# Modulation of both layers in the first phase of a two-layer diffusion trunk

## The reference

```python
def _adaln(cond, ada_w, ada_b):
    m = jax.nn.silu(cond) @ ada_w + ada_b          # (1024,) @ (1024, 6144)
    return jnp.split(m[:, None, :], 6, axis=-1)
...
for i in range(DEPTH):                              # DEPTH = 2
    sh1p, sc1p, g1p, sh2p, sc2p, g2p = _adaln(c_ctx[None, :], ada_w[i], ada_b[i])
    sh1s, sc1s, g1s, sh2s, sc2s, g2s = _adaln(c, ada_w[i], ada_b[i])
```

## Time and profile before

| | |
|---|---|
| median of three runs | 4691.73 us (4690.29 to 4693.51) |
| profiled execution, span | 4690.2 us |
| the profiled execution's own time beside its span | not given apart; the three runs are 0.1 to 3.3 us above the span |
| TensorE busy | 4009.3 us (85%) |
| VectorE busy | 1621.5 us (35%) |
| first phase, up to the first load of norm 0 | 125.2 us |
| route of layer 0, first load to first expert matmul | 1105.64 to 1287.24 us |
| route of layer 1, first load to first expert matmul | 3678.74 to 3825.10 us |

### The profile page before, as it was taken

The page is one execution under the profiler, slowest core; times in us unless marked ns, Lnnn a source line. Parts: engine busy times, 40 slices in busy tenths (PEclk is TensorE's granted clock), DMA queues, the critical chain, the costliest instruction groups (busy, mean ns, idle before and its releaser), DMA issues. The chain is left out here.

```text
span 4690.2 us, 56580 instructions
## 1 busy us (share of the span) xinstructions
PE 4009.3 (85%) x22791; PEld 3241.3 (69%) x22791; DVE 1621.5 (35%) x2557; ACT 926.8 (20%) x1606; POOL 582.8 (12%) x446
## 2 busy tenths in 40 slices
PE   8599798977799999995999956877888649999996
PEld 1599543454299999995999943444444549999995
DVE  3432355443600010014125546566666351000101
ACT  0423202013111111114123322111111301111112
POOL 0000000000200010000001103343344001000100
PEclk9699797987899999997999977888888669999998
DMA  6422201046667787753222255111110538778774
GB/s 222 158 66 62 105 11 50 15 160 250 224 235 271 274 274 260 269 180 112 85 73 84 65 180 202 45 45 49 63 50 27 192 105 278 256 268 282 259 271 172
DMA packets 342007, 732.47 MB, mean 156 GB/s; under 512 B 17220, under 2 KB 59708, under 8 KB 335986
## 3 DMA queue, kind: packets, MB, share of 16 engines
q1 hardware_dynamic: 306028, 625.59, 37.5%
q0 software_dynamic: 27168, 99.25, 7.6%
q10 hardware_dynamic: 8719, 6.51, 0.5%
HBM read 635.71 MB, written 95.59 MB: 156 GB/s over the span
## 5 line engine op out<-in xcount | busy, mean ns | idle before, releaser
L1608 PE MATMUL moe_banks<-moe_xt,mix_ring 128*128 128x144 f32 x8192 | 1012.7, 287 | 3.3 <-ACT moe_xt L1646 3.3
L1608 PEld LDWEIGHTS moe_banks<-moe_xt,mix_ring 128*128 128x128 f32 x8192 | 1009.0, 191 | 4.0 <-issue 3.5
L1623 PE MATMUL moe_banks<-moe_hid,mix_ring 128*128 128x144 f32 x4096 | 510.3, 287 | 0.0
L1623 PEld LDWEIGHTS moe_banks<-moe_hid,mix_ring 128*128 128x128 f32 x4096 | 503.5, 191 | 0.9
L1671 DVE TENSOR_TENSOR moe_hid<-moe_banks,moe_sg 128x144 f32<-128x144 f32 x256 | 78.8, 308 | 921.9 <-ACT moe_sg L1657 921.9
L62 PE MATMUL ssdin_banks<-h_leading,ssdin_w_split 128*128 128x384 f32 x1920 | 385.8, 335 | 5.8 <-ACT ssdin_pad L1867 2.9
L62 PEld LDWEIGHTS ssdin_banks<-h_leading,ssdin_w_split 128*128 128x128 f32 x1920 | 337.4, 188 | 7.2 <-issue 7.0
L1657 ACT ACTIVATE moe_sg<-moe_banks 128x144 f32<-128x144 f32 x256 | 74.3, 290 | 964.0 <-PE moe_banks L1608 964.0
L2553 DVE SCALAR_TENSOR_TENSOR scan_exp<-scan_exp,scan_rates,scan_cb 128x128 f32<-128x128 f32 x576 | 240.4, 490 | 56.4 <-ACT scan_exp L2444 55.9
L2346 PE MATMUL scan_banks<-scan_w,scan_yc 128*128 128x512 f32 x576 | 251.9, 599 | 4.4 <-DVE scan_yc L2596 4.4
L62 PE MATMUL hyin_banks<-h_leading,hyin_w_split 128*128 128x384 f32 x1152 | 235.5, 339 | 19.2 <-DVE hyin_w_split L575 18.9
(11 more groups left out here) (335 smaller groups left out, 4602.3 us busy)
## 6 DMA issues: line engine op xcount, KB each, us to landing
mix_ring<-in_moe_w_gate SPq DMA_DIRECT2D x64, 2048.0 KB, 7.8
mix_ring<-in_moe_w_up SPq DMA_DIRECT2D x64, 2048.0 KB, 12.9
mix_ring<-in_moe_w_down SPq DMA_DIRECT2D x64, 2048.0 KB, 9.3
mod_w<-in_ada_w SPq DMA_DIRECT2D x12, 2048.0 KB, 7.9
mix_ring<-in_ada_w SPq DMA_DIRECT2D x12, 2048.0 KB, 15.9
ssdin_w<-in_ssd_in_w SPq DMA_DIRECT2D x10, 2048.0 KB, 9.9
scan_xbc<-xbc_dram SPq DMA_DIRECT2D x9, 1536.0 KB, 7.0
st_xb<-xbc_dram SPq DMA_DIRECT2D x10, 1280.0 KB, 7.1
```

What stands on the lines that cost most here:

```text
L1608: ins = pe.matmul(pb[:, 2 * (f % 2) + j, 0:SLOTS], ring[:, 2 * half + j, k, col:col + P], xt[:, k, :], start=(k == 0), stop=(k == KD - 1))
L1623: ins = pe.matmul(pb[:, d % 4, 0:SLOTS], ring[:, 4 + half, k, col:col + P], hid[:, k, :], start=(k == 0), stop=(k == KD - 1))
```

## The change

Both layers' modulation is computed in the first phase. Its ring has six buffers instead of three. The 24 products are written out one after another in three banks, always in partitions 0 and 1; a product waits for the bank that the product three before it used, and filter layer 1 runs behind product 8. The rows of layer 0 are in partitions 0 and 1 and those of layer 1 in partitions 32 and 33 of the same tile, into which the bias is loaded first. Layer 0's rows are stored when all pieces have been issued, layer 1's behind its last piece; four read-backs follow, with four transposes and four column copies. `NextModulation` is gone and the route of layer 0 is the code of the route of layer 1.

```diff
--- before.py
+++ after.py
@@ -117,18 +117,20 @@
 def phase_modulation(nc, io, keep):
     ada = io["ada_w"].rearrange("l (k p) n -> p l k n", p=P)
-    RING = 3
+    RING = 6
     COLUMNS = 6 * D // HALF
+    ALL = 2 * COLUMNS
+    BANKS = (1, 2, 3)
+    FIRST = 9
     with ExitStack() as ctx:
         m = Mem(nc, ctx, "mod_")
         cond_rows = m.sb("cond_rows", [16, P])
         cond_t = keep["cond_t"]
         w = m.sb("w", [P, RING, KD, HALF])
-        bias = m.sb("bias", [2, 6 * D])
-        rows = m.sb("rows", [2, 6 * D])
-        a_row = m.sb("a_row", [2, D])
-        gain = m.sb("gain", [2, D])
-        mrows = m.sb("mrows", [48, 2, P])
+        rows = m.sb("rows", [34, 6 * D])
+        a_row = m.sb("a_row", [34, D])
+        gain = m.sb("gain", [34, D])
+        mrows = m.sb("mrows", [48, 4, P])
         stage = m.sb("stage", [P, 4, P])
         filt = Filter(m, io, keep["filt"])
         pb = m.psum()
@@ -147,28 +149,38 @@
         s_tr = m.sem("param_transposed")
         s_done = m.sem("params_kept")
+        def of_layer(tile, layer):
+            return tile[32 * layer:32 * layer + 2, :]
+
         with nc.Block() as block:
             @block.sync
             def _(sp):
+                def piece(n):
+                    layer, col = n // COLUMNS, n % COLUMNS
+                    sp.dma_start(w[:, n % RING, :, :], ada[:, layer, :, col * HALF:(col + 1) * HALF]).then_inc(s_w[n % RING], 16)
                 sp.dma_start(cond_rows[0:8, :], io["c_ctx"].rearrange("(k p) -> k p", p=P)).then_inc(s_c, 16)
                 sp.dma_start(cond_rows[8:16, :], io["c"][0].rearrange("(k p) -> k p", p=P)).then_inc(s_c, 16)
                 filt.load(sp)
-                for r in range(RING):
-                    sp.dma_start(w[:, r, :, :], ada[:, 0, :, r * HALF:(r + 1) * HALF]).then_inc(s_w[r], 16)
-                with sp.Fori(1, COLUMNS // RING) as i:
-                    for r in range(RING):
-
-                        sp.wait_ge(s_acc, i * RING + (r - RING + 1))
-                        sp.dma_start(w[:, r, :, :], ada[:, 0, :, bass.ds((i * RING + r) * HALF, HALF)]).then_inc(s_w[r], 16)
-                sp.wait_ge(s_row, COLUMNS)
-                sp.wait_ge(s_arow, 1)
-                modulation_out(sp, io, 0, rows, a_row, mrows, s_out, s_back)
+                for n in range(ALL):
+                    if n >= RING:
+                        sp.wait_ge(s_acc, n - RING + 1)
+                    piece(n)
+                for layer in range(2):
+                    sp.wait_ge(s_row, COLUMNS * (layer + 1))
+                    sp.wait_ge(s_arow, layer + 1)
+                    modulation_out(sp, io, layer, of_layer(rows, layer), of_layer(a_row, layer), s_out)
+                for layer in range(2):
+                    sp.wait_ge(s_out, 2 * 5 * 16)
+                    for c in range(2):
+                        sp.dma_start(mrows[:, 2 * layer + c, :], io["mod_dram"][layer, c].rearrange("(r p) -> r p", p=P)
+                                     ).then_inc(s_back, 16)
             @block.scalar
             def _(act):
-                modulation_in(act, io, 0, bias, gain, s_bias)
+                for layer in range(2):
+                    modulation_in(act, io, layer, of_layer(rows, layer), of_layer(gain, layer), s_bias)
                 for n, (src, at, cnt) in enumerate(keep["param_rows"]):
                     act.dma_start(stage[at[1]:at[1] + cnt, at[0], :], src).then_inc(s_stage, 16)
                 for h in range(2):
@@ -184,53 +196,68 @@
             @block.tensor
             def _(pe):
+                def product(n):
+                    pe.wait_ge(s_w[n % RING], 16 * (n // RING + 1))
+                    if n >= len(BANKS):
+                        pe.wait_ge(s_row, n - len(BANKS) + 1)
+                    for k in range(KD):
+                        ins = pe.matmul(pb[0:2, BANKS[n % len(BANKS)], :], cond_t[:, k, :], w[:, n % RING, k, :],
+                                        start=(k == 0), stop=(k == KD - 1))
+                    ins.then_inc(s_acc, 1)
+
                 pe.wait_ge(keep["s_const"], 16)
                 pe.wait_ge(s_c, 32)
                 pe.transpose(pb[:, 0, 0:16], cond_rows[:, :], keep["ident"][0:16, 0:16]).then_inc(s_ct, 1)
                 pe.wait_ge(s_silu, 2)
-                for layer in range(2):
-
-                    filt.products(pe, pb, layer)
-                    with pe.Fori(layer * COLUMNS // RING // 2, (layer + 1) * COLUMNS // RING // 2) as i:
-                        for r in range(RING):
-
-                            pe.wait_ge(s_w[r], i * 16 + 16)
-
-                            pe.wait_ge(s_row, i * RING + (r - RING + 1 if layer else 0))
-                            for k in range(KD):
-                                ins = pe.matmul(pb[0:2, 1 + r, :], cond_t[:, k, :], w[:, r, k, :],
-                                                start=(k == 0), stop=(k == KD - 1))
-                            ins.then_inc(s_acc, 1)
+                filt.products(pe, pb, 0)
+                for n in range(FIRST):
+                    product(n)
+                filt.products(pe, pb, 1)
+                for n in range(FIRST, ALL):
+                    product(n)
                 pe.wait_ge(filt.s_arg, 2)
                 pe.wait_ge(s_stage, 16 * (len(keep["param_rows"]) + 2))
                 for n, cnt in enumerate(keep["param_counts"]):
                     pe.transpose(pb[:, 4 + n // 4, (n % 4) * P:(n % 4) * P + cnt], stage[0:cnt, n, :],
                                  keep["ident"][0:cnt, 0:cnt]).then_inc(s_tr, 1)
-                pe.wait_ge(s_back, 32)
-                for c in range(2):
+                pe.wait_ge(s_back, 64)
+                for c in range(4):
                     pe.transpose(pb[:, 6, c * P:c * P + 48], mrows[:, c, :], keep["ident"][0:48, 0:48]).then_inc(s_tr, 1)
             @block.vector
             def _(dve):
                 ch = Chain(dve, s_dve)
+
+                def collect(n):
+                    layer, col = n // COLUMNS, n % COLUMNS
+                    at = slice(col * HALF, (col + 1) * HALF)
+                    dve.wait_ge(s_acc, n + 1)
+                    dve.tensor_tensor(of_layer(rows, layer)[:, at], pb[0:2, BANKS[n % len(BANKS)], :],
+                                      of_layer(rows, layer)[:, at], ALU.add).then_inc(s_row, 1)
+
+                def gains(layer):
+                    dve.wait_ge(s_row, COLUMNS * (layer + 1))
+
+                    dve.scalar_tensor_tensor(of_layer(a_row, layer), of_layer(rows, layer)[:, 4 * D:5 * D], 1.0,
+                                             of_layer(gain, layer), ALU.add, ALU.mult).then_inc(s_arow, 1)
+
                 ch.link(dve.memset(keep["eps"][:, :], EPS))
-                dve.wait_ge(s_bias, 64)
-                for layer in range(2):
-                    filt.angles(dve, pb, layer)
-                    with dve.Fori(layer * COLUMNS // RING // 2, (layer + 1) * COLUMNS // RING // 2) as i:
-                        for r in range(RING):
-                            dve.wait_ge(s_acc, i * RING + (r + 1))
-                            at = bass.ds((i * RING + r) * HALF, HALF)
-                            dve.tensor_tensor(rows[:, at], pb[0:2, 1 + r, :], bias[:, at], ALU.add).then_inc(s_row, 1)
-                dve.wait_ge(s_row, COLUMNS)
-
-                dve.scalar_tensor_tensor(a_row[:, :], rows[:, 4 * D:5 * D], 1.0, gain[:, :], ALU.add, ALU.mult).then_inc(s_arow, 1)
-                dve.wait_ge(s_tr, 6)
+                filt.angles(dve, pb, 0)
+                dve.wait_ge(s_bias, 128)
+                for n in range(FIRST):
+                    collect(n)
+                filt.angles(dve, pb, 1)
+                for n in range(FIRST, ALL):
+                    collect(n)
+                    if n % COLUMNS == COLUMNS - 1:
+                        gains(n // COLUMNS)
+                dve.wait_ge(s_tr, 4)
                 for n, cnt in enumerate(keep["param_counts"]):
                     dve.tensor_copy(keep["prm"][:, n, 0:cnt], pb[:, 4 + n // 4, (n % 4) * P:(n % 4) * P + cnt]
                                     ).then_inc(s_done, 1)
-                modulation_columns(dve, keep, 0, pb[:, 6, :], s_done)
+                dve.wait_ge(s_tr, 8)
+                modulation_columns(dve, keep, pb[:, 6, :], s_done)
 def modulation_in(eng, io, layer, bias, gain, s_bias):
@@ -240,26 +267,25 @@
         eng.dma_start(gain[c:c + 1, :], io["norm_g"][layer, 1:2, :]).then_inc(s_bias, 16)
-def modulation_out(sp, io, layer, rows, a_row, mrows, s_out, s_back):
+def modulation_out(sp, io, layer, rows, a_row, s_out):
     for which, src in ((V_G1, 2), (V_B2, 3), (V_G2, 5)):
         sp.dma_start(io["vec_dram"][layer, :, which, :], rows[:, src * D:(src + 1) * D]).then_inc(s_out, 16)
     sp.dma_start(io["vec_dram"][layer, :, V_A2, :], a_row[:, :]).then_inc(s_out, 16)
     sp.dma_start(io["mod_dram"][layer], rows[:, :]).then_inc(s_out, 16)
-    sp.wait_ge(s_out, 5 * 16)
-    for c in range(2):
```

(63 more changed lines are left out.)

62 lines of the change are left out of this document (removed).

## The result

The changed kernel takes 4740.11 us (median of four runs, 4731.83 to 4740.41) against 4691.83 us for the kernel before (four runs beside it): a ratio of 1.0097, 95% interval 1.0085 to 1.0109. It is slower by 1.0%. Forecast were 4739.1 us and a range of 4729 to 4752 us. The profiled execution has a span of 4738.6 us against 4690.2 us before, 48.4 us more; forecast were 4737.6 us and 47.4 us more.

The account below looks back on a forecast made before the run. TensorE, not DMA, was taken to pace the first phase: +83.0 us there and -35.6 us in route and first expert give +47.4 us, span 4737.6 us. With the timed runs' median 1.5 us above: 4739.1 us, range 4729 to 4752 us.

Parts of the forecast that it names:

- The twelve products: First phase: layer 1's twelve products add 6.87 us each with no other work to hide them, 82.4 us.
- The waits around piece 2 and 3: First phase: pieces 1 and 2 still late from DMA, piece 3 no longer waits for VectorE, 0.9 us saved.
- ScalarE's later start: First phase: four more loads delay filter and product 0 by 1.45 us, absorbed by piece 1's wait; cost 0.3 us.
- third rival: First phase: six queued pieces get ahead of q10's packets, piece 2's wait and clock dip vanish; 4733 us, chance 0.05.
- The tail: End of first phase: doubled read-backs, transposes, copies and gains, less earlier parameter copies; 1.2 us more, bounds 0.5 and 3.
- The first phase together: First phase: products, piece 3's wait, later start and tail sum to +83.0 us.
- Route 0: Layer 0's route: its three stretches become as long as layer 1's, 26.64 + 0.00 + 8.60 = 35.24 us saved.
- The experts' first 256 matmuls: Behind layer 0's route: half of a difference in when the clock rises, 0.4 us saved, bounds 0 and 0.9.
- The ring kept up: First phase, rival: the ring does not keep up, later pieces late at 4.5 us each; 4753 to 4762 us, chance 0.08.
- Route 0 came down in full: Layer 0's route, rival: it does not come down to layer 1's, only 27.5 us come back; 4747 us, chance 0.08.
- No slower: First phase, rival: products follow DMA's pace, break-even at 2.9 us a piece; 4709 us at 5.4 us; chance 0.02.
- the prediction's figure of 1.85 us for each wait: First phase: each wait for DMA also lowers the clock, costing 1.85 us beyond the wait itself.

Follow-up runs that it names:

- e2: The changed kernel without layer 1's twelve piece loads and products, its bias loads, stores, read-backs and transposes kept; 4652.98 us, ratio 0.9913 to the kernel before.
- e1: The changed kernel with a ring of three buffers in place of six; 4739.89 us, ratio 1.0096 to the kernel before.
- e4: The changed kernel with each product's eight steps of k dealt to four output partition pairs, VectorE adding four partial rows; 4695.33 us, ratio 1.0003.
- e5: The kernel before with a written-out first phase of twelve products, a ring of six and k over four partition pairs; 4672.81 us, ratio 0.9955.
- e3: The changed kernel with the two d_skip loads issued behind ScalarE's second sine in place of the start; 4740.18 us in one run.
- e6: e5 with route 0's twelve products moved behind the last tile, in three groups of four, each product in its own partition pair; 4657.95 us, ratio 0.9925.
- e7: e6 with the two skip weight loads issued behind the last product of the first phase; 4658.76 us, ratio 0.9922.
- e10: e6 with the skip weights loaded in the long convolution; 4647.45 us, ratio 0.9909.
- e11: e10 with route 0's products in four groups of three in place of three groups of four; 4641.73 us, ratio 0.9897.

## Why the prediction was right

**The twelve products.** Forecast 82.4 us. The last row comes 194.84 - 114.33 = 80.51 us later. The blocks give 6.88 us a piece, 12 x 6.88 = 82.6 us; e2, which takes just these products out, has the last row 81.48 us sooner. The pace and the claim that nothing hides them held; what the last row lacks to 82.6 us are the smaller terms that follow.

**The waits around piece 2 and 3.** Forecast was -0.9 us for piece 3, and it came. Piece 2 starts 0.97 us later (39.47 against 38.50 us), of which forecast was 0.3 us. The reason given there failed: piece 1's wait did not take up ScalarE's later start. The first product starts 1.53 us later (19.85 against 18.32 us), the wait for piece 1 is still 1.54 us, and piece 1 starts 1.95 us later; it is the wait for piece 2 that got shorter, by 0.98 us. The first product of the kernel before:

```profile
18.32 8.90 PE L201 MATMUL mod_banks<-mod_w,cond_t 128*2 128x512 f32 x16
```

Against that stands something not in the sum: piece 2 takes 6.89 us in place of 8.72 us, because the clock doesn't fall behind its wait of 1.67 us. 82.6 - 0.9 + 1.0 - 1.8 = 80.9 us, against 80.51 us measured. Half of the third rival came true: the dip went and the waits stayed, so its mechanism (six queued pieces get ahead of q10's packets) is not what happened; e1, with three queued, has no dip either.

**The tail.** Forecast 1.2 us more, measured 11.71 - 10.89 = 0.82 us. SP's four read-backs take 1.70 us in place of 0.77 us for two, 0.93 us more where 0.77 us were forecast; the other parts of this sum together came out smaller than forecast.

**The first phase together.** Forecast +83.0 us, measured 206.55 - 125.22 = +81.33 us; the clock dip is the largest part of the miss.

**Route 0.** Forecast -35.24 us, measured 146.51 - 181.60 = -35.09 us. The three stretches of layer 1's route (70.28, 61.97, 14.11 us) were met by 70.72, 61.91 and 13.88 us, and the cast took 0.22 us. The experts' first 256 matmuls: forecast -0.4 us, measured 33.67 against 33.88 us, -0.2 us.

**The rest.** Some 2.2 us more lie in phases and parts that don't differ in code: norm 0 +0.4, hyena and convolution together +0.7, SSD in +0.6, states -1.2, scan +0.4, final norm +0.5 us and smaller ones. No one of them is beyond what it scatters by between kernels. The forecast had put these at nothing, so that its hit to 1 us is in part luck: the first phase grew 1.7 us less than forecast, and these made up for it.

**The rivals.** The ring kept up, and e1 shows that three buffers would have. (The rival's lowest time is 4753 us; the stated range ends at 4752 us, just short of the edge it is said to take in.) Route 0 came down in full. No slower: e4 shows that the condition named (pieces at the DMA's pace) gives back 34.8 us of the first phase, and that even then 171.73 - 125.22 = 46.5 us are paid there for the 35 us saved in the route. The rival's 4709 us for that case was about right: 4695.33 us were measured, and 12.0 us of the difference are the scan's. So placing all 24 pieces in the first phase loses by its loads alone: 24 pieces at 5.42 us are 130 us, half of them had been loaded beside other work, and e5 against e4 shows these twelve at 67.0 us.

## What to carry to other kernels

Moving work out of a phase that hides most of it into one that hides none costs its full length: of 95.1 us of TensorE work only 35 us had been on the path. Before moving a product, see how much of the array it uses; a stationary operand of two columns leaves room for three more products in other partitions, and that cut a piece from 6.88 to 1.90 us at the full clock. Then the loads are the bound, and it matters more where they stand: keep loads of four-byte elements away from large loads and from short round trips through DRAM, since they cost 11 to 14 us in either place and nothing in a stretch without traffic.

## What the runs showed of the hardware

**Small packets against large.** While 2019 packets of four bytes ran beside 2235 of the pieces, the rate was 189 GB/s, without them 386 GB/s (e3). What they hit depends on what is in flight: pieces at the start (11 us of the last product's time once TensorE is fast, e6 against e7), a store of 48 KB at the end (16.45 us in place of 3.03 us).

**The clock and short waits.** A wait of 2.65 us before piece 2 was followed by 0.50, waits of 1.67 us and 1.90 us were not. In e4 pauses of 1.4 to 3.5 us at most pieces left the clock going between its levels, mean 0.74, and the same 16 records took 1.90 or 3.59 us. The length of the wait alone does not decide: 2.50 us in e2 and 2.65 us before were followed by the low clock, but in e10 a wait of 3.53 us was not,

```profile
31.07 1.90 PE L193 MATMUL mod_banks<-mod_w,cond_t 128*2 128x512 f32 x16 [3.53 <-DMA mod_w<-in_ada_w]
```

while the next one there, of 3.52 us, was (0.50 from 36.5 to 38 us, the piece took 3.38 us). So the prediction's figure of 1.85 us for each wait holds for piece 2 of the kernel before and not for waits in general; what decides stays open. Nor does the recorded clock explain every slow piece: e4's piece 0 took 3.59 us at 20.17 us, where the rows grant 1.00.

**Two lengths of the scan.** The scan of layer 1 has the same code in all kernels. In the profiled executions it took 833.5 to 833.9 us before, after and in most others, 832.1 us in e11, but 821.49 us in e2 and 821.87 us in e4. The group of VectorE's that differs, first after the change, then in e4:

```profile
L2460 DVE SCALAR_TENSOR_TENSOR scan_exp<-scan_exp,scan_rates,scan_cb 128x128 f32<-128x128 f32 x576 | 232.8, 479 | 65.3 <-ACT scan_exp L2351 64.8
```

```profile
L2465 DVE SCALAR_TENSOR_TENSOR scan_exp<-scan_exp,scan_rates,scan_cb 128x128 f32<-128x128 f32 x576 | 209.8, 438 | 85.4 <-ACT scan_exp L2356 85.1
```

576 instructions of 479 ns against 438 ns: 23 us of VectorE. They do not set the phase by themselves: before, they took 240.4 us (490 ns) in a scan of 833.5 us, in e1 229.7 us (471 ns) in one of 833.9 us. POOL works beside them, and goes the other way: its 32 instructions on the tile `state` take 1608 ns each before, 1719 ns after, 1763 ns in e1 and 2070 ns in e4, where VectorE's take 490, 479, 471 and 438 ns. The Trainium skill, page "SBUF — State Buffer", section "Who interferes with whom", ties such slowing to a port that VectorE and GpSimd share; that would fit, but no run here takes POOL's work away, so the cause is only argued. Why one kernel falls into the one length and another into the other stays open. For reading these comparisons it means that a difference of 12 us in the total may be the scan's, and has to be looked up by phase, as for e2 and e4.
